# The opening of a six-layer, one-core fp32 kernel: one fused stage in place of four, with the inputs in order of first need

## The reference, cut to what matters

```
h = rms_norm(x, attn_norm[0])                   # x * rsqrt(mean(x*x) + 1e-6) * gain
proj = h @ w_in[0]                              # of it, the 672 MLA columns first (c_q, c_kv, k_pe)
ang = positions * freqs; cos, sin = cos(ang), sin(ang)       # rope tables, used from the MLA part on
silu_c = silu(c)                                # conditioning of the second network
lb = softmax(hg_lb_logits over layers)[1]       # used in the second network's layer 1
```

## Time and profile before

| | us |
|---|---|
| median of three runs | 2781.19 (2779.69 to 2784.41) |
| the profiled execution, its own time | 2794.67 |
| span of its trace (first to last instruction) | 2792.6 |
| PE busy / weight loads (PEld) / DVE / ACT / POOL, us of the span | 2467.0 / 2340.1 / 2009.3 / 1411.4 / 106.8 |
| DMA, mean over the span | 166 GB/s |
| first TensorE instruction of the projection, us from the span's start | 42.18 |

### The profile page before, as it was taken

How to read it: one execution, slowest core, us unless ns; L and a number is a source line. 1 busy time by engine, 2 the same in 40 slices (tenths; PEclk the granted TensorE clock), 3 DMA queues, 4 the chain that set the end, 5 groups by cost and what they waited for, 6 DMA issues and landing times. The chain is left out here.

```text
span 2792.6 us, 46473 instructions
## 1 busy us (share of the span) xinstructions
PE 2467.0 (88%) x18832; PEld 2340.1 (84%) x18832; DVE 2009.3 (72%) x3340; ACT 1411.4 (51%) x2536; POOL 106.8 (4%) x103
## 2 busy tenths in 40 slices
PE   3888999988889999767999979998987999976997
PEld 3678999977789999756998879997787999855997
DVE  3465788754757787696887768886458788757885
ACT  4542555355434554525764566646554664434663
POOL 0010000000100000440000000000001000000000
PEclk9799999998999999888999999999989999988999
DMA  4021656741216568411555724573333457621452
GB/s 190 31 91 48 226 208 259 298 185 53 84 68 228 219 242 324 159 45 66 191 220 213 277 92 150 188 295 116 142 121 136 151 188 295 257 76 61 170 193 76
DMA packets 63365, 462.89 MB, mean 166 GB/s; under 512 B 7024, under 2 KB 7088, under 8 KB 7216
## 3 DMA queue, kind: packets, MB, share of 16 engines
q1 hardware_dynamic: 62640, 456.16, 44.2%
q10 hardware_dynamic: 512, 3.77, 0.4%
HBM read 458.85 MB, written 1.05 MB: 165 GB/s over the span
## 5 line engine op out<-in xcount | busy, mean ns | idle before, releaser
L749 PE MATMUL psum<-arena_rounded,upper_rounded 128*128 128x256 f32 (+1 forms) x5208 | 1489.6, 286 | 139.4 <-PEq L651 49.5
L750 PE MATMUL psum<-arena_rounded,upper_rounded 128*128 128x256 f32 (+1 forms) x5208 | 1474.7, 283 | 0.0
L751 PE MATMUL psum<-arena_rounded,ring_rounded 128*128 128x256 f32 (+1 forms) x5208 | 1474.2, 283 | 0.0
L749 PEld LDWEIGHTS psum<-arena_rounded,upper_rounded 128*128 128x128 f32 (+1 forms) x5208 | 998.0, 192 | 160.2 <-issue 81.5
L566 DVE TENSOR_TENSOR ring_rounded<-ring,upper_rounded 128x1024 fp32r<-128x1024 f32 (+4 forms) x960 | 846.8, 901 | 356.1 <-ACT upper_rounded L557 352.0
L557 ACT ACTIVATE upper_rounded<-ring 128x1024 fp32r<-128x1024 f32 (+4 forms) x960 | 752.0, 793 | 640.9 <-PE psum L751 555.6
L750 PEld LDWEIGHTS psum<-arena_rounded,upper_rounded 128*128 128x128 f32 (+1 forms) x5208 | 999.9, 192 | 1.5 <-issue 1.4
L751 PEld LDWEIGHTS psum<-arena_rounded,ring_rounded 128*128 128x128 f32 (+1 forms) x5208 | 1000.6, 192 | 0.1
L588 DVE SCALAR_TENSOR_TENSOR ada_sum<-ring,small,ada_sum 128x1024 f32<-128x1024 f32 x168 | 214.7, 1278 | 1.3
L2394 DVE SCALAR_TENSOR_TENSOR arena<-psum,cols,arena 128x255 f32<-128x255 f32 (+1 forms) x352 | 153.2, 477 | 72.4 <-ACT arena L2361 69.3
L2361 ACT ACTIVATE arena<-psum,cols 128x256 f32<-128x256 f32 x176 | 89.5, 561 | 78.4 <-PE psum L751 78.3
(11 more groups left out here) (513 smaller groups left out, 2484.6 us busy)
## 6 DMA issues: line engine op xcount, KB each, us to landing
ring<-stream_dram SPq DMA_DIRECT2D x434, 1024.0 KB, 4.9
const<-const_dram ACTq DMA_DIRECT2D x1, 1607.0 KB, 7.2
x<-x_dram ACTq DMA_DIRECT2D x1, 1024.0 KB, 9.2
out_dram<-x SPq DMA_DIRECT2D x1, 1024.0 KB, 4.8
cols<-cols_dram ACTq DMA_DIRECT2D x1, 982.0 KB, 10.5
pos<-positions_dram ACTq DMA_DIRECT2D x1, 64.0 KB, 11.2
```

The lines of the kernel that those rows point to most:

```text
L749: pe.matmul(out, upper, x[0][:, b.k, :], start=(b.k == 0), stop=False)
L750: pe.matmul(out, upper, x[1][:, b.k, :], start=False, stop=False)
L751: ins = pe.matmul(out, lower, x[0][:, b.k, :], start=False, stop=(b.k == nk - 1))
```

## The change

One fused stage (`first_block`) takes the place of the four. In it:

- SP's queue issues, in this order: x; the first 134 columns of const (`FIRST`: ones, the epsilons and the angles' three columns, which are moved to the front); the first 8 columns of cols (the norm's gains); positions; units 0 and 1; the rest of cols; the rest of const; units 2 to 5. Each has a semaphore of its own.
- In `first_norm`, DVE first clears a 128x256 tile `zeros`. TensorE runs 5 matmuls on it before the sums and 4 after them. ACT runs one Ln on it before x has landed. While TensorE sums, DVE computes the angles (the same instructions without the last copy), ACT writes the upper part of chunk 0, and DVE its lower part. After the root, DVE computes lower k-1 right behind product k, and the splits of chunks 1 to 3 stand between the tiles: ACT's behind upper 0, 2 and 4, DVE's behind lower 1, 3 and 5.
- `conditioning` puts the sine, the Silu and the Exp on ACT in `mla_latents` at i = 0, between `act_step(0)` and the copies of tile 0; DVE's first half comes after `dve_step(0)`, and its second half (which waits for the Exp) after `dve_step(2)`. TensorE waits for the rest of const before the fold, and DVE for the sine before the rope rows.

```diff
+FIRST = P + 6
...
+def load_inputs(chip, st, x_in, cols_in, const_in, positions):
...
+    @st.block.sync
+    def _(sp):
+        sp.dma_start(chip.x[:, :], x_in).then_inc(x_loaded, 16)
+        sp.dma_start(chip.const[:, 0:FIRST], const_in[:, 0:FIRST]).then_inc(first_loaded, 16)
+        sp.dma_start(chip.cols[:, 0:KD], cols_in[:, 0:KD]).then_inc(gains_loaded, 16)
+        sp.dma_start(chip.pos[D_NOPE:P, :], positions.broadcast_to([P - D_NOPE, T])).then_inc(pos_loaded, 16)
+        for u in range(2):
+            chip.load_unit(sp, u)
+        sp.dma_start(chip.cols[:, KD:], cols_in[:, KD:]).then_inc(cols_loaded, 16)
+        sp.dma_start(chip.const[:, FIRST:], const_in[:, FIRST:]).then_inc(const_loaded, 16)
+        for u in range(2, RING):
+            chip.load_unit(sp, u)
...
     @block.tensor
     def _(pe):
+        pe.wait_ge(zeros_ready, 1)
+        for _ in range(5):
+            pe.matmul(chip.bank(0, T), zeros[:, 0:P], zeros, start=True, stop=True)
+        pe.wait_ge(first_loaded, 16)
         for k in range(KD):
             pe.wait_ge(squared, k + 1)
             ins = pe.matmul(chip.bank(2, T), chip.con("ones"), squares[:, k, :], start=(k == 0), stop=(k == KD - 1))
         ins.then_inc(var_ready, 1)
+        for _ in range(4):
+            pe.matmul(chip.bank(0, T), zeros[:, 0:P], zeros, start=True, stop=True)
 
     @block.scalar
     def _(act):
+        act.wait_ge(zeros_ready, 1)
+        act.activation(chip.small[:, 168:169], zeros[:, 0:1], ACT.Ln, bias=1.0)
+        act.wait_ge(x_loaded, 16)
         for k in range(KD):
             act.activation(squares[:, k, :], xs[:, k, :], ACT.Square, scale=1.0 / 32).then_inc(squared, 1)
+        w.act(act, -1, 1)
+        act.wait_ge(first_loaded, 16)
         act.wait_ge(var_ready, 1)
         root_of(chip, act, rstd, chip.bank(2, T), RMS_EPS, root_ready)
         for k in range(KD):
             act.wait_ge(whole_ready, k + 1)
             act.activation(chip.rounded(upper[:, k, :]), lower[:, k, :], ACT.Identity).then_inc(upper_ready, 1)
+            w.act(act, -1, 2 + k // 2)
 
     @block.vector
     def _(dve):
+        chain = Chain(dve, dve_chain)
+        dve.memset(zeros, 0.0).then_inc(zeros_ready, 1)
+        dve.memset(chip.cos[0:lo, :], 1.0)
+        dve.wait_ge(first_loaded, 16)
+        dve.wait_ge(pos_loaded, 16)
+        chain(dve.tensor_copy(ang, chip.pos[lo:hi, :]))
...
+        dve.tensor_scalar(table, table, -PI, PI, ALU.max, ALU.min).then_inc(angles_ready, 1)
+        w.dve(dve, -1, 1)
...
+        dve.wait_ge(gains_loaded, 16)
         dve.wait_ge(root_ready, 2)
         for k in range(KD):
             dve.scalar_tensor_tensor(lower[:, k, :], xs[:, k, :], gain(k), rstd, ALU.mult,
                                      ALU.mult).then_inc(whole_ready, 1)
-        for k in range(KD):
-            dve.wait_ge(upper_ready, k + 1)
...
+            if k:
+                lower_of(k - 1)
+                w.dve(dve, -1, 1 + k // 2)
+        lower_of(KD - 1)
...
+    def on_act(act):
+        act.wait_ge(angles_ready, 1)
+        act.activation(table, table, ACT.Sin).then_inc(cosines_ready, 1)
+        act.wait_ge(cols_loaded, 16)
+        act.activation(chip.silu_c, chip.col("c", 0, KD), ACT.Silu)
+        act.wait_ge(shifted, 1)
+        act.activation(shares, shares, ACT.Exp).then_inc(exps_ready, 1)
...
             for i in range(steps):
                 s["act_step"](act, i)
+                if opening and i == 0:
+                    opening[0](act)
                 if i == 3:
                     load_roots(chip, act)
...
                 s["dve_step"](dve, i)
+                if opening and i == 0:
+                    opening[1](dve)
+                if opening and i == 2:
+                    opening[2](dve)
+            if opening:
+                dve.wait_ge(opening[4], 1)
...
+        if opening:
+            opening[3](pe)
         pe.wait_ge(free, 6)
...
+def first_block(chip, *inputs):
+    with fused(chip) as st:
+        loaded = load_inputs(chip, st, *inputs)
+        out = chip.place(H0, KD, T), chip.place(H0_LOW, KD, T)
+        x_ready, waits = first_norm(chip, st, lambda k: chip.col(("attn_norm", 0), k), out, loaded)
+        mla_latents(chip, st, 0, x_ready, conditioning(chip, st, *waits))
```

More of the change, by code:

```diff
@@ L361, in shape_constants @@
     parts = {
+        "ones": np.ones((P, P)),
+        **{("eps", e): np.full((P, 1), e) for e in (RMS_EPS, LN_EPS, GN_EPS)},
+        "freq": np.zeros((P, 1)),
+        "quarter": np.where((p >= D_NOPE) & (p < D_QK), 0.25, 0.0),
+        "right_angle": np.where((p >= D_NOPE) & (p < D_QK), np.pi / 2, 0.0),
         "ident": p == f,
-        "ones": np.ones((P, P)),
         "heads": p // D_RW == f // D_RW,
@@ L371, in shape_constants @@
         "sel": np.zeros((P, H_ML * P + 2 * H_ML)),
[L372 to L375, removed]
     }
@@ L1089, in _, with conditioning, on_dve, bounds @@
                                      ALU.mult).then_inc(whole_ready, 1)
-        for k in range(KD):
-            dve.wait_ge(upper_ready, k + 1)
-            dve.tensor_tensor(chip.rounded(lower[:, k, :]), lower[:, k, :], chip.whole(upper[:, k, :]),
-                              ALU.subtract).then_inc(lower_ready, 1)
-    return lower_ready
+            if k:
+                lower_of(k - 1)
+                w.dve(dve, -1, 1 + k // 2)
+        lower_of(KD - 1)
+    return lower_ready, (angles_ready, cols_loaded, const_loaded)
+def conditioning(chip, st, angles_ready, cols_loaded, const_loaded):
+    table = chip.cos[D_NOPE:P, :]
+    logits = chip.col("lb", 0, L2 * KD).rearrange("p (l c) -> p l c", c=KD)
+    shares = chip.small[:, 72:104].rearrange("p (l c) -> p l c", c=KD)
+    top = chip.small[:, 104:112]
+    shifted, exps_ready, cosines_ready, dve_chain = st.signals("shifted", "exps_ready", "cosines_ready", "bounds_chain")
+    def on_act(act):
[5 more added lines that the diff above has]
+        act.activation(shares, shares, ACT.Exp).then_inc(exps_ready, 1)
+    def on_dve(dve):
+        chain = Chain(dve, dve_chain)
+        dve.wait_ge(cols_loaded, 16)
+        chain(dve.tensor_tensor(top, logits[:, 0, :], logits[:, 1, :], ALU.max))
+        for l in range(2, L2):
+            chain(dve.tensor_tensor(top, top, logits[:, l, :], ALU.max))
+        dve.tensor_tensor(shares, logits, over(top, L2), ALU.subtract).then_inc(shifted, 1)
+    def bounds(dve):
+        chain = Chain(dve, dve_chain)
+        chain.counts[dve_chain.num] = L2 - 1
+        dve.wait_ge(exps_ready, 1)
+        chain(dve.tensor_tensor(top, shares[:, 0, :], shares[:, 1, :], ALU.add))
+        for l in range(2, L2):
+            chain(dve.tensor_tensor(top, top, shares[:, l, :], ALU.add))
+        chain(dve.reciprocal(top, top))
+        chain(dve.tensor_tensor(chip.lb, shares[:, 1, :], top, ALU.mult))
+        dve.tensor_scalar(chip.lb_rest, chip.lb, -1.0, 1.0, ALU.mult, ALU.add)
+    def on_pe(pe):
+        pe.wait_ge(const_loaded, 16)
+    return on_act, on_dve, bounds, on_pe, cosines_ready
 def plain_project(chip, name, rhs, nk, dst):
@@ L1115, in mla_places, with mla_latents @@
     return upper, k, pe_square, pe_turned
-def mla_latents(chip, st, l, x_ready):
+def mla_latents(chip, st, l, x_ready, opening=None):
     h = chip.split(chip.place(H0, KD, T), chip.place(H0_LOW, KD, T))
@@ L2142, in merge_branches @@
             mla_latents(chip, st, l + 1, x_ready)
-def first_layer(chip, l):
-    if l == 0:
-        with fused(chip) as st:
-            out = chip.place(H0, KD, T), chip.place(H0_LOW, KD, T)
-            x_ready = first_norm(chip, st, lambda k: chip.col(("attn_norm", l), k), out)
-            mla_latents(chip, st, l, x_ready)
+def first_block(chip, *inputs):
[4 more added lines that the diff above has]
+        mla_latents(chip, st, 0, x_ready, conditioning(chip, st, *waits))
+def first_layer(chip, l):
     mla_branch(chip, l)
```

106 lines of the change are left out of this document (31 added, 75 removed).

## The result

The changed kernel takes 2746.36 us, the median of four runs (2745.76 to 2757.21), against 2781.99 us before (2779.69 to 2784.41): 35.6 us less, a ratio of 0.9881 (95% interval 0.9855 to 0.9907). The forecast was 2757.0 with a range of 2750 to 2766. The way was right, and the size was half as large again as forecast. The profiled execution took 2757.21 us, its span is 2755.3 us.

The account below looks back on a forecast made before the run. TensorE, idle behind a non-overlapping opening chain (transfers, angles and conditioning, norm, split), was taken as the bound. Chunk 4 26.5 us earlier, less 2.5 for half clock, saves 24.0: 2781.2 - 24.0 = 2757 us, range 2750 to 2766.

Parts of the forecast that it names:

- lost to the half clock in chunks 4 and 5: TensorE, chunks 4 and 5: after 6.2 us idle, 5 us at half clock, losing 2.5 us.
- sum of the opening: TensorE starts chunk 4 at 30.4 instead of 56.93 us, 26.5 us earlier; less 2.5 for half clock, 24.0 us.
- Rival (b): Norm's sums at old speed (+1.9 us), unit 0 or positions late (up to 1); 2759 to 2760; chance 0.19.
- DVE now sets the pace: From root to tile 7, DVE is the bound: 8.8 us plus 0.6 waiting; product 7 ends at 21.9 us.
- rival (a): TensorE's gap ahead of chunk 4 does not lower the clock, or is short; saving 26.5, time 2754.7 us; chance 0.14.
- (c): Transfers share the DMA engines and x lands at 9.9 us as before: +3.9, 2761 us; chance 0.11.
- (d): Table switches ahead of tile 0's copy cost twice: three times 1.3 us more, 2761 us; chance 0.04.
- (e): Unit 3 lands after 48.4 us, delaying tile 0's copies; about 2787 us if at 54; chance 0.03.
- I take the saving as the same in both: 2781.2 - 24.0 = 2757: Whole kernel: the 24.0 us saved on the profiled execution (2794.67) applies to the runs' median, giving 2757 us.
- from there on the old trace, 24 us earlier: Behind TensorE's start on chunk 4 and its half clock, later stages run as before, shifted 24 us.
- the other bounds: Range's low end, 2750: 4 us below a 26.5 us saving, for x at 5.5, run spread, shorter DVE phase.
- gives back or adds more than 3 us: Sign of failure: a stage after chunk 4's start shifts differently by over 3 us, something not costed.

Follow-up runs that it names:

- e1: The changed kernel once more, unaltered; its runs go from 2745.1 to 2757.0 us.
- e9: The changed kernel a third time, unaltered, with more runs; median 2751.85 us.
- e10: The changed kernel with its two sets of semaphores exchanged, with more runs; median 2752.44 us.
- e12: The changed kernel with every transfer issued about 1.9 us later, behind six clears on DVE; mean 2751.8 us.
- e4: The kernel before with the change's nine matmuls on zeros in its first stage; mean 2779.7 us.
- e5: The changed kernel without its nine matmuls on zeros; mean 2752.3 us.

## Why the prediction was wrong

The opening, step by step, against the changed kernel's first profile:

| step | forecast | measured |
|---|---|---|
| x landed | 6.0 | 5.5 |
| positions landed | 6.5 | 8.0 |
| unit 0 landed | 9.1 | 10.4 |
| the norm's sums, on a raised clock | 3.7 us long | 3.69 us |
| root ready | 12.5 | 13.6 |
| TensorE starts chunk 0 | 13.8 | 15.25 |
| chunk 3 ended | 24.2 | 28.0 |
| conditioning ahead of tile 0's copy | 4.7 us long | 4.76 us |
| TensorE starts chunk 4 | 30.4 | 31.38 |
| TensorE idle before chunk 4 | 6.2 us | 3.37 us |
| lost to the half clock in chunks 4 and 5 | 2.5 us | 1.65 us |
| **earlier at the latents' sums** | **24.0 us** | **23.9 us** |

**The sum of the opening was right, with two errors against each other.** Unit 0 landed 1.3 us later than by the count, with three small transfers between x and it (that they are the reason is not shown), and through the split of chunk 0, which I had put ahead of the root, this made the root 1.1 us late. Rival (b) named this wait, but not for its first reason, since the sums did run on a raised clock. Against it, TensorE ran the first 17 matmuls of chunk 0 at half clock after an idle stretch of 3.70 us, so that chunk 3 ended late, the gap before chunk 4 was short, and less was lost there. "DVE now sets the pace" did not hold either: TensorE never waited between 15.25 and 28.0 us. The sum had chunk 3 end 10.4 us after the start on chunk 0, but 96 matmuls take 11 us even at full clock, by its own 5.5 us for 48; here they took 12.8. Seen over several profiles the loss ahead of the latents' sums comes and goes: in e1 TensorE waited 3.37 us as well, and the sums came at 37.02 us, without it. The stretch in question in the changed kernel and in e1:

```profile
31.38:36.00 4.62, 4.62 (x26) 4.62 (x27) 1.04 (x4) 3.43 (x10) 0.00 (x0) 0.63 0.23 98
```

```profile
31.38:36.00 4.62, 4.51 (x40) 4.54 (x40) 1.21 (x6) 4.47 (x12) 0.00 (x0) 1.00 0.24 99
```

That is rival (a), but in e1 alone. In e9, e10 and e12 chunk 0 ran at full clock, TensorE then waited longer ahead of chunk 4 (4.8, 4.5 and 4.8 us from start to start), and ran at half clock for some 6 us from there on, much as forecast. In e9:

```profile
14.60:18.00 3.40, 3.23 (x26) 3.08 (x27) 2.97 (x7) 2.34 (x5) 0.00 (x0) 1.00 0.99 422
...
30.60:36.00 5.40, 5.32 (x25) 5.35 (x26) 1.10 (x4) 3.48 (x9) 0.00 (x0) 0.50 0.27 112
```

The mean of five profiles with this opening is 38.6, that of four with the old one 62.6: 24.0 us. Rivals (c), (d) and (e) did not occur.

**The step that failed is the last one:** "I take the saving as the same in both: 2781.2 - 24.0 = 2757". It puts everything behind the opening at nothing ("from there on the old trace, 24 us earlier"), with a range that gave 4 us to "the other bounds (x at 5.5, the spread of the runs, a shorter DVE phase)". Two things were wrong in it.

First, three runs between 2779.7 and 2784.4 looked like a narrow kernel. It is not: 64 executions lie between 2768.5 and 2792.2, and even the difference of 13.5 us between the profiled execution and the median, which I noted and passed over, said so. The means are 2780.55 and 2750.28, a difference of 30.3 us (standard error 1.5). The 35.6 us between the two medians hold 5.3 us more than that, and those are luck: the 2746.36 of the first four executions lies 3.9 us below the mean of fourteen, and the 2781.99 of before 1.4 above the mean of 64.

Second, the rest of the program did not stay the same. Of the 30.3 us only 24.0 are seen at the latents' sums; some 6 us are gained behind them, 3.3 of these beside POOL's masks. The prediction's own sign of being wrong, a later part that "gives back or adds more than 3 us", is met. An allowance for the spread alone would hardly have reached the result: 6 us below 2757 is 2751.

**What stays open.** 24 us are shown, by one mark per run. The 6 us behind it are four standard errors, if executions are independent, and every kernel with the new opening shows a gain there. The place beside POOL's masks repeats in all fifteen profiles, but its cause is not shown: the constants moved by six columns with the change, and no run has the new opening with the constants in their old place, or the other way round. For the other 3 us there is no place: the pair with exchanged sets differs by 24.2 us in total (standard error 2.7), which leaves room for the semaphores' sets as well as for nothing. The place of TensorE's instructions is no likely cause (e4). The pace could not be set from the kernel, so no run holds it fixed.

## What to carry to other kernels

When TensorE idles behind a chain of loads, set-up and barriers, count forward from zero in the order of first need, engine by engine, and find the next place where an engine is asked for moved work: here moved table switches took 4.8 us in front of a PSUM copy, and two of them with a third load fitted into a wait of the next stage. Moving them is worth less than they take: 2.5 us at the latents' sums. A barrier also waits for a queue that only issues. A later stage whose instructions stay the same need not keep its time, as the masks' place shows: compare single instructions over all profiles of either kind before calling a difference scatter. Before forecasting a change of 1%, ask how far executions of the same program lie apart: three runs don't say, and a profile that differs by 0.5% from the median is a warning; compare a mark in the traces that the scatter does not reach.

## What the runs showed of the hardware

TensorE at full granted clock and never idle has two lasting paces for 128x256 matmuls of this kind, each with a weight load of its own: 885 or 851 in 100 us, or 113.3 and 117.8 ns from start to start. In short pieces the traces also have 111.7 ns. The pace can change inside a stretch without idle time, behind a single distance of about 200 ns (in the first profiles of both kernels from 113.5 to 118 ns, behind one of 201 ns), and at the same place of the program it differs between executions. The Trainium skill, "TensorE: Matmul & The Clock Gate", section "Wait — 56ns, not 53.3ns?", gives the columns divided by 2.4 GHz plus about 2.5 ns for matmuls back to back; an estimate by that is 109.2 ns for 256 columns. No lasting stretch here is that quick, so the measured ones decide.

Matmuls on a tile of zeros bring TensorE to its full pace as others do (0.43 us from start to start up to 5.19 us in the changed kernel, 0.22 after that; the sums take 3.69 us with the zeros and 6.70 without them in e5). The same idle stretch of 3.37 us ahead of chunk 4 was followed by half clock in the changed kernel's first profile and not in e1. And the same DVE and POOL instructions, running beside each other, took 2.6 and 7.3 to 7.9 us in the five profiles with the old opening and 2.2 to 2.3 and 6.1 to 6.8 in the ten with the new one; the DVE instruction alone takes 0.48 us in both.
